# A two-part transformer network on one core: where the modulation rows are summed over the partitions

## What is computed

```python
sc, scc = silu(c), silu(c_ctx)                      # 1024 values each
for l in range(2):
    mod = sc @ w_mod[l] + b_mod[l]                  # 1024 x 6144, a row of 6144 values
    sh1, sc1, g1, sh2, sc2, g2 = split(mod, 6)
    u = rms_norm(h, norm1_g[l]) * (1 + sc1) + sh1
    if l == 0:                                      # the context has its own row
        csh1, csc1, ... = split(scc @ w_mod[l] + b_mod[l], 6)
        uc = rms_norm(ctx, norm1_g[l]) * (1 + csc1) + csh1
    h = h + g1 * mixer(u, uc)
    h = h + g2 * sq_relu_mlp(rms_norm(h, norm2_g[l]) * (1 + sc2) + sh2, w_mlp1[l], w_mlp2[l])
```

## Time and profile before

| | |
|---|---|
| time, median of 3 runs | 1562.83 us (1562.11 to 1563.29) |
| profiled execution, span from first to last instruction | 1560.5 us |
| PE busy | 1523.2 us, 98% |
| DVE busy | 1164.3 us, 75% |
| ACT busy | 785.1 us, 50% |
| POOL busy | 9.6 us, 1% |
| bytes moved by DMA | 311.57 MB, mean 200 GB/s |

### The profile page before, as it was taken

One profiled execution on the slowest core, in us unless ns is written; L12 is line 12 of the kernel. 1 busy time (PEld: TensorE's weight loads), 2 busy tenths in 40 slices (PEclk: granted clock), 3 DMA queues, 4 the chain that ended last, 5 costly groups with the idle time before them and its releaser, 6 DMA issues.

```text
span 1560.5 us, 28953 instructions
## 1 busy us (share of the span) xinstructions
PE 1523.2 (98%) x11842; PEld 1463.9 (94%) x11842; DVE 1164.3 (75%) x1675; ACT 785.1 (50%) x1127; POOL 9.6 (1%) x15
## 2 busy tenths in 40 slices
PE   7999999999999999999989999999999999899998
PEld 7999998999999899999769999987799999899998
DVE  7887788978877858787767877774768887686563
ACT  5444458643435633445765343454654544454542
POOL 0000000000000100000000000000000000000000
PEclk9999999999999999999999999999999999999999
DMA  7656652646664537666233666643345767336540
GB/s 286 230 225 261 228 221 91 243 154 249 226 253 187 226 114 284 250 236 249 81 135 109 263 250 248 247 161 135 102 149 219 268 265 274 136 126 226 189 163 28
DMA packets 43735, 311.57 MB, mean 200 GB/s; under 512 B 4848, under 2 KB 5104, under 8 KB 6512
## 3 DMA queue, kind: packets, MB, share of 16 engines
q1 hardware_dynamic: 42048, 303.33, 51.7%
q0 software_dynamic: 1008, 5.73, 1.0%
q10 hardware_dynamic: 576, 1.05, 0.2%
HBM read 309.05 MB, written 1.05 MB: 199 GB/s over the span
## 4 chain that ended last, share of the span: by engine, by line
PE 67%; DVE 10%; ACT 3%; issue 1%; DVEq 0%; ACTq 0%
PE psum L1822 18%; PE psum L1828 18%; PE psum L1829 18%; DVE w_lo L1025 5%; PE psum L2066 3%; PE psum L2072 3%; PE psum L2071 3%; DVE buf L1034 2%; ACT w_hi L491 2%; PE psum L1899 1%; DVE buf L1195 1%; PE psum L2385 1%; PE psum L2396 0%; PE psum L2315 0%; DVE buf L1198 0%
## 5 line engine op out<-in xcount | busy, mean ns | idle before, releaser
L1822 PE MATMUL psum<-u_hi,w_hi 128*128 128x256 f32 (+1 forms) x2288 | 658.1, 288 | 17.1 <-DVE u_lo L1117 9.6
L1025 DVE TENSOR_TENSOR w_lo<-raw,w_hi 128x1024 fp32r<-128x1024 f32 x480 | 564.5, 1223 | 115.6 <-ACT w_hi L491 115.4
L1828 PE MATMUL psum<-u_lo,w_hi 128*128 128x256 f32 (+1 forms) x2288 | 650.1, 284 | 0.0
L1829 PE MATMUL psum<-u_hi,w_lo 128*128 128x256 f32 (+1 forms) x2288 | 649.9, 284 | 0.0
L491 ACT ACTIVATE w_hi<-raw 128x1024 fp32r<-128x1024 f32 x480 | 477.3, 1046 | 71.0 <-PE psum L1822 59.0
L1822 PEld LDWEIGHTS psum<-u_hi,w_hi 128*128 128x128 f32 x2288 | 440.9, 193 | 21.5 <-DVE w_lo L1025 9.7
L1828 PEld LDWEIGHTS psum<-u_lo,w_hi 128*128 128x128 f32 x2288 | 441.0, 193 | 0.4
L1829 PEld LDWEIGHTS psum<-u_hi,w_lo 128*128 128x128 f32 x2288 | 440.8, 193 | 0.0
L1822 PE MATMUL psum<-hid_hi,w_hi 128*128 128x256 f32 x1220 | 346.2, 284 | 1.8 <-issue 1.2
L1828 PE MATMUL psum<-hid_lo,w_hi 128*128 128x256 f32 x1220 | 345.2, 283 | 0.0
L1829 PE MATMUL psum<-hid_hi,w_lo 128*128 128x256 f32 x1220 | 345.1, 283 | 0.0
(11 more groups left out here) (261 smaller groups left out, 1048.5 us busy)
## 6 DMA issues: line engine op xcount, KB each, us to landing
raw<-stream SPq DMA_DIRECT2D x288, 1024.0 KB, 5.0
buf<-tab POOLq DMA_DIRECT2D x2, 768.0 KB, 5.3
x<-x_in SPq DMA_DIRECT2D x2, 512.0 KB, 6.8
buf<-ctx_in POOLq DMA_DIRECT2D x1, 1024.0 KB, 9.4
buf<-poolmat POOLq DMA_DIRECT2D x1, 1024.0 KB, 5.3
out<-x ACTq DMA_DIRECT2D x4, 256.0 KB, 2.5
cst<-consts POOLq DMA_DIRECT2D x1, 864.0 KB, 9.0
buf<-late POOLq DMA_DIRECT2D x1, 640.0 KB, 4.2
```

The source lines that it names most:

```text
L1025: ve.tensor_tensor(w_lo[:, u], raw[:, u], w_hi[:, u].bitcast(F32), ALU.subtract).then_inc(S.lo_ready, 1)
L1822: ins = te.matmul(dst, w_hi[:, w], hi, start=first, stop=False, skip_group_check=True)
L1828: te.matmul(dst, w_hi[:, w], lo, start=False, stop=False, skip_group_check=True)
L1829: return te.matmul(dst, w_lo[:, w], hi, start=False, stop=last, skip_group_check=True)
```

## The change

The sums over the partitions go from PE to POOL. For each group POOL waits until DVE has accumulated its last unit, makes one `partition_all_reduce` of the accumulator into a new tile `mod_row` (128 x 512, every partition holds the sum), waits for it, and issues a DMA of one row of `mod_row` to 128 partitions, four values each, into `mod`. It waits for the landing before the next sum. Context sums go the same way. So that the four values are neighbours, the columns of the modulation's weight units are stored in another order, and `mod` has another layout. PE's sums and all its waits on the modulation go; DVE's reads of PSUM go, and the bias is added later in seven instructions over many columns (`add_bias`), behind waits for the DMAs. The accumulators alternate from group to group. ACT gets waits before `buf[0]` is overwritten. Constants that nothing uses (`headsum`, `headbc`) go from the program and from the DMA of constants.

```diff
-        MOD_ACC[_g] = _i % 2 if _name == "mlp0" else int(_i >= len(_groups) - 3)
+        MOD_ACC[_g] = _g % 2
...
-CC = {"ident": 0, "ones": 128, "tri": 256, "headsum": 384, "stick": 512, "colmask": 896, "headbc": 960}
-NCONST = CC["headbc"] + NC * P
+CC = {"ident": 0, "ones": 128, "tri": 256, "stick": 384, "colmask": 768}
+NCONST = CC["colmask"] + HD
...
+        mod_row = sb("mod_row", 512)
...
-        mod = mod_t[:, :].rearrange("p (l j c) -> p l j c", l=2, c=2)
+        mod = mod_t[:, :].rearrange("p (l c j) -> p l j c", l=2, c=2)
...
             # POOL
+            def group_sum(acc, done, count, dst, landed, landings):
+                gp.partition_all_reduce(mod_row[:, :], acc, P, bass.bass_isa.ReduceOp.add).then_inc(done, 1)
+                pool.wait_ge(done, count)
+                pool.dma_start(dst, mod_row[0:1, :].rearrange("o (p m) -> o p m", m=4)).then_inc(landed, 16)
+                pool.wait_ge(landed, 16 * landings)
+
+            def sum_groups(name):
+                for g in HOME[name]:
+                    l, at = GROUPS[g][0], 4 * GROUPS[g][1]
+                    pool.wait_ge(S.lo_ready, last_unit(g) + 1)
+                    group_sum(mod_acc[MOD_ACC[g]], S.mod_summed, g + 1, mod[:, l, at:at + 4, 0], S.mod_in, g + 1)
+                    for f in range(2):
+                        if g == CTX_GROUPS[f][-1]:
+                            for n in range(2):
+                                at = 4 * GROUPS[CTX_GROUPS[f][n]][1]
+                                group_sum(ctx_acc[n], S.ctx_summed, 2 * f + n + 1, mod[:, 0, at:at + 4, 1], S.ctx_mod_in, 2 * f + n + 1)
...
+                if name == "ffn0":
+                    sum_groups("ffn0")
                 if name == "ctx":
                     pool.wait_ge(S.acc_ready, 4 * ACC["wout"] + 4)
                     pool.dma_start(buf[3][:, :], ctx_in).then_inc(S.ctx_in, 16)
+                    sum_groups("ffn1")
                 if name == "woe":
+                    sum_groups("ffn2")
+                    sum_groups("ffn3")
                     pool.wait_ge(S.acc_ready, 4 * ACC["ffn3"] + 4)
                     pool.dma_start(buf5[:, 0:NLATE], late).then_inc(S.late_in, 16)
...
+                    sum_groups("mlp0")
...
             # ACT, before the convolution, and before the queries are copied
+            act.wait_ge(S.mod_summed, HOME["ffn0"][-1] + 1)
+            act.wait_ge(S.ctx_summed, 2)
...
+            act.wait_ge(S.mod_summed, HOME["ffn2"][-1] + 1)
...
             # DVE
-                    if j in SUM_AT[name]:
-                        read_modulation(HOME[name][SUM_AT[name].index(j)])
...
-            read_context_modulation(1)
-            modulation_done("ffn1")
-            dve.wait_ge(S.ctx_read, 2)
+            modulation_in(HOME["ffn1"][-1])
+            dve.wait_ge(S.ctx_mod_in, 16 * 4)
+            add_bias(0, 0, 32)
+            add_bias(0, 0, 16, 1)
...
-            modulation_done("ffn3")
+            modulation_in(HOME["ffn3"][-1])
+            add_bias(0, 32, 48)
+            add_bias(1, 0, 24)
...
-            modulation_done("mlp0")
+            modulation_in(HOME["mlp0"][3])
+            add_bias(1, 24, 40)
...
+            modulation_in(HOME["mlp0"][-1])
+            add_bias(1, 40, 48)
             update_x("mlp1", lambda k: part(1, 5, k))
...
             # PE
-                    if j in SUM_AT[name]:
-                        g = groups[SUM_AT[name].index(j)]
-                        sum_modulation(g, 0, last_unit(g))
...
-                if name in ("ffn0", "ffn1"):
-                    sum_context(int(name[3]))
...
-    mods = w["w_mod_2"].reshape(2, 4, 2, P, 12, 512).transpose(0, 4, 1, 3, 2, 5).reshape(-1, P, UNIT)
+    mods = w["w_mod_2"].reshape(2, 4, 2, P, 12, 4, P).transpose(0, 4, 1, 3, 2, 6, 5).reshape(-1, P, UNIT)
```

More of the change, by code:

```diff
@@ L210, in __init__ @@
         self.mod_summed = sem("mod_summed")
-        self.mod_read = sem("mod_read")
+        self.mod_in = sem("mod_in")
+        self.mod_biased = sem("mod_biased")
         self.ctx_summed = sem("ctx_summed")
-        self.ctx_read = sem("ctx_read")
+        self.ctx_mod_in = sem("ctx_mod_in")
         self.dve_chain = sem("dve_chain")
@@ L448, in sum_squares, with last_unit @@
                 gp.tensor_tensor(buf[4][:, 0:T], buf[4][:, 0:T], buf[4][:, T:2 * T], ALU.add).then_inc(S.ctx_ssq, 1)
+            def group_sum(acc, done, count, dst, landed, landings):
[3 more added lines that the diff above has]
+                pool.wait_ge(landed, 16 * landings)
+            def last_unit(g):
+                return max(c for c, (group, _) in MOD_UNIT.items() if group == g)
+            def sum_groups(name):
[8 more added lines that the diff above has]
+                                group_sum(ctx_acc[n], S.ctx_summed, 2 * f + n + 1, mod[:, 0, at:at + 4, 1], S.ctx_mod_in, 2 * f + n + 1)
             pool.wait_ge(S.hi_ready, 4)
@@ L960, in _ @@
             sc.preload_act_table_set("sqrt_and_others")
-            act.wait_ge(S.mod_read, HOME["mlp0"][-1] + 1)
+            act.wait_ge(S.mod_biased, 1)
             shift_operand(1)
@@ L1050, in modulate @@
                 if ctx and q == 0 and f == 1:
-                    dve.wait_ge(S.ctx_summed, 1)
+                    dve.wait_ge(S.ctx_summed, 2)
                 n = CTX_GROUPS[f].index(g) if ctx else None
@@ L1225, in context_operand, with add_bias, modulation_in @@
                                             u_hif[:, k - 1, T:2 * T], ALU.add, ALU.subtract).then_inc(S.ctx_lo, 1)
[L1227 to L1246, removed]
+            def add_bias(l, at, end, c=0):
+                link(ve.tensor_tensor(mod[:, l, at:end, c], mod[:, l, at:end, c],
+                                      prm[:, COL["bmod"] + 48 * l + at:COL["bmod"] + 48 * l + end], ALU.add))
+            def modulation_in(last):
+                dve.wait_ge(S.mod_in, 16 * (last + 1))
             def scale_gain(dst, l, n, gain, c=0):
@@ L1719, in _ @@
             sqrelu("mlp0")
-            modulation_done("mlp0")
+            modulation_in(HOME["mlp0"][3])
+            add_bias(1, 24, 40)
+            dve.sem_inc(S.mod_biased, 1)
             scale_gain("H2", 1, 4, "n2_1")
@@ L1887, in diagonal_block @@
                 ins.then_inc(done, 1)
[L1889 to L1898, removed]
-                    ins = te.matmul(psum[:, bank, at + 2 * m:at + 2 * m + 2], mod_acc[acc][:, m * P:(m + 1) * P],
-                                    ones[:, 0:2], start=m == 0, stop=True, skip_group_check=True)
-                ins.then_inc(S.mod_summed, 1)
-            def sum_context(f):
-                unit_ready(last_unit(CTX_GROUPS[f][1]))
-                pe.wait_ge(S.mod_read, HOME[f"ffn{f}"][-1] + 1)
-                for m in range(8):
-                    ins = te.matmul(psum[:, 6, 8 + 2 * m:10 + 2 * m], ctx_acc[m // 4][:, (m % 4) * P:(m % 4 + 1) * P],
-                                    ones[:, 0:2], start=m == 0, stop=True, skip_group_check=True)
-                ins.then_inc(S.ctx_summed, 1)
             def up(c, i, j, bank, h0):
@@ L1920, in swiglu @@
             def swiglu(name, norm, free=lambda: None):
-                c0, h0, groups = AT[name], STEPS[name], HOME[name]
+                c0, h0 = AT[name], STEPS[name]
                 def down(j, slot, c, i=0, first=False, last=False):
@@ L1952, in swiglu @@
                         down(j - 2, s, c + 3, 2 * i)
-                        if s == 2:
-                            sum_modulation(groups[-3] + i, 1, unit_at(name, "mod", 13), 2 * i)
                 down(FFS - 2, (FFS - 2) % 4, end_of(name) - 2)
-                if name in ("ffn0", "ffn1"):
-                    sum_context(int(name[3]))
                 down(FFS - 1, (FFS - 1) % 4, end_of(name) - 1, last=True)
@@ L1968, in up_pair @@
                         pe.wait_ge(S.up_scaled, h0 + max(j - 1, 3))
-                    if j - 2 in SUM_AT[name]:
-                        pe.wait_ge(S.mod_read, HOME[name][SUM_AT[name].index(j - 2)] + 1)
                     all_k(c, 0, psum[:, bank, 0:TS], w=TS)
@@ L1998, in sqrelu @@
                     down(j - 1)
-                    if j in SUM_AT[name]:
-                        g = HOME[name][SUM_AT[name].index(j)]
-                        pe.wait_ge(S.up_scaled, h0 + j + 1)
-                        sum_modulation(g, MOD_ACC[g], last_unit(g), bank=4 + 2 * (j % 2), at=MOD_COL)
                 down(MLS - 1, last=True)
@@ L2011, in _ @@
             pe.wait_ge(S.ms_ready, NRM["ffn0"] + 1)
-            pe.wait_ge(S.ctx_read, 1)
             def gate_chunk(k, done):
@@ L2107, in _ @@
             pe.wait_ge(S.k_cols_read, 1)
-            pe.wait_ge(S.ctx_read, 2)
             project_tokens("v", 4, lambda b: None, {4: turn_keys})
@@ L2239, in _ @@
                 ins.then_inc(S.acc_ready, 1)
-            pe.wait_ge(S.mod_read, HOME["ffn3"][-1] + 1)
             for k in range(NC):
@@ L2554, in shape_constants @@
     cst[:, CC["tri"]:CC["tri"] + P] = p[:, None] >= p[None, :]
-    for m in range(NC):
```

(4 more changed lines are left out.)

10 lines of the change are left out of this document (removed).

## The result

The changed kernel takes 1565.33 us in the median of 20 runs, the kernel before 1562.89 in 20 runs beside them: ratio 1.0014, 95% interval 1.0008 to 1.0020. That is 2.4 us slower, and lies within the 0.2% that the prediction calls no change; the forecast was 23 us faster. The profiled execution has a span of 1564.0 us, 3.5 more than the earlier trace rows.

A forecast was written before the change was run, and what follows sets the result against it. PE was taken to bound the five stages; its 24.6 us less what DVE takes back gave 23, and 1560.5 - 23 + 2.3 = 1540 us, range 1535 to 1665.

The forecast's parts named there:

- What is removed: PE's 28 sums in the five stages: 0.88 us each, 24.6 us in all.
- What is added on POOL: 28 reductions on POOL at 1.3 to 2 us, each followed by a 2 KB DMA landing after 3 us, hidden.
- the rival of POOL's queue: POOL bounds the kernel from 19 us a sum in the second block; about 2100 us; with longer holds 0.16.
- What the reduction does to DVE: In the five stages, DVE and POOL exclude each other at SBUF; each reduction costs DVE about its hold, 1.3 to 2 us.
- About h us: DVE's loss for each reduction in the five stages, h being how long the reduction holds its input.
- What DVE can spare: Stage length less DVE's busy time and two ACT waits a step: 16.5, 16.5, 19.4, 29.0, 15.3 us in the five stages.
- the prediction's own rule: Each stage's change is the larger of minus PE's share and (sums x h - spare); balance lost at about 3.2 us.
- no gain: Five stages: at holds of 3.0 to 3.3 us PE's 24.6 us return as DVE's waits; 1560 to 1566; chance 0.07.
- DVE becomes the bound: Five stages: holds over 3.2 us make DVE fall behind; 1600 at 4.7, 1662 at 7; chance 0.29 for 3.3 to 7.
- What would show it: Signs in the five stages; right: POOL's sums under 3 us; wrong: subtractions' mean up by tenths, DVE busy over 90%.

## Why the prediction was wrong

*What is removed* was right: every sum shows as -0.88 us, and the run with 16 columns is 25.1 us faster, where 24.6 was worked out. The bias additions are six, not seven, of 0.17 us each.

*What is added on POOL* was too low for the instruction and nearly right for what counts, its hold. The instruction takes 3.22 us, where 1.3 to 2 was taken; it holds DVE for 2.1 of them. The 2 KB row lands 1.9 us after its issue (3 was taken), and no engine waits for POOL anywhere; the rival of POOL's queue fell with that, and with it the estimate of 62 us by the Trainium skill, page "GPSIMD Engine Reference", section "Cross-partition — where GPSIMD wins": this instruction takes a twentieth of it.

*What the reduction does to DVE*: the lock was right, the price too high. "About h us" for each of 28 would be 59; it was 33, because 21 of the sums begin beside a scaling that reads PSUM and a wait for ACT. The prediction had priced no such cover. One unit later, where this cover is gone, the excess was 56 us.

*What DVE can spare* is the step that failed. The prediction took the stage's length less DVE's busy time less "the two waits on ACT that stand in each step"; the earlier trace rows shows the third one, 115.6 us before L1025, and it was left out. In the five stages it is 8.1, 8.6, 11.8, 11.8 and 9.5 us: half of the 97 us counted as spare. What is left besides is partly outside the steps, as the norms at the ends of stages. With the waits for PE alone as spare time, and the excess from the trace (4 x 1.18 + 2 x 2.04 = 8.8 in each of the first two blocks; 3 x 1.18 + 2 x 1.99 = 7.5; 2 x 1.19 + 3 x 0.44 = 3.7; 2.5 + 5 x 0.63 = 5.7), the prediction's own rule gives +0.5, +0.5, +3.0, -4.4 and +2.7, together +2.3 us. The table's first row has -0.5, -0.5, +3.7, -1.2 and +0.8, together +2.3. The sum agrees better than its parts do, and that is in part luck. In the fourth block the rule is 3 us too hopeful, since of its waits for PE all but 4.2 us came behind 930, after the two dearest reductions (882 and 902); that their order is the reason is argued, not tried. In the third block the 8.7 us behind the block's end are left out, and the measured sum contains a slower clock (below) that the rule knows nothing of.

The kernel before with reductions of constants shows that the rule is rough. There the reductions stretch DVE by 7.5, 7.4, 7.5, 3.7 and 5.7 us, of which the rule would make 0, 0, 3.0, 0 and 2.7; the table has +2.4, +2.3, +2.6, +2.7 and +3.8. A part is a wait that the changed kernel doesn't have, of PE's own sums for DVE's accumulation (1.0, 0.9, 1.4 and 1.4 us in the four swiglu blocks), and in the fourth a stretch of the slower clock; but in the first two blocks PE waits 0.9 us each for a subtraction too, where the excess is under the spare time. What is shown, then, is that much less than 97 us was to spare; how much of the waits for PE can be used is open. With 2.1 us for every sum and the right spare time the rule would have given +21, or 1584, the time of the run with later reductions.

A second, smaller part is that a wait of PE can cost more than its length. Behind four gaps in PE's products of 2.1 to 3.4 us (at 733, 905, 1202 and 1342) the granted clock fell to the lower of its two levels, 1.2 GHz; in windows of the changed kernel (us; busy of PE, PEld, DVE, ACT, POOL; clock, where 1.00 is 2.4 GHz):

```profile
738.20:741.50 3.30, 3.30 (x17) 3.30 (x16) 3.02 (x7) 2.86 (x7) 0.00 (x0) 0.50 0.56 238
908.90:912.20 3.30, 3.30 (x17) 3.30 (x17) 2.78 (x5) 0.42 (x1) 0.00 (x0) 0.50 0.93 377
1205.80:1209.10 3.30, 3.30 (x17) 3.30 (x17) 3.30 (x4) 1.25 (x2) 0.00 (x0) 0.50 0.33 89
1345.80:1349.10 3.30, 3.30 (x17) 3.30 (x17) 0.00 (x0) 0.00 (x0) 0.00 (x0) 0.50 0.07 27
```

At 733 two products start 3.38 us apart, 3.26 more than usual, and the step in the pairing is 4.79, so the slow stretch behind it cost about 1.5 us more. The kernel before has one such stretch in these stages, 0.50 from 1198.4 to 1201.7, so three are new: at 1.5 us each an estimate of 4 to 5 us that a sum over DVE's lateness doesn't contain. Behind a gap of 2.14 us at 620 it stayed at 1.00, so the length of the gap alone doesn't say it. This was read from the trace and not tried by itself.

*The rivals.* What came was "no gain", which had 0.07, and not for its reason: its condition was a hold of 3.0 to 3.3 us, the hold was 2.1. "DVE becomes the bound" had the mechanism, but its point of decision, 3.2 us, was worked out from the same wrong spare time: with the waits for PE in its place the rule is in balance at about 1.2 us a sum, and 33.3 / 28 = 1.2 is what a sum cost.

*What would show it*: the subtractions' mean rose by 0.016 us, not by tenths, and DVE was busy 82 to 84% of the first three stages; neither is a sign of "wrong" by the prediction's list. Two of its other marks told: POOL's sums took 3.22 us, where "under 3" was to stand for right, and PE waited 16.9 us for the low halves of weights.

## What to carry to other kernels

Before an engine's idle time is called spare, sort it by what ended it: a wait for a third engine in program order is as spent as work, and at most what it waits for the engine that sets the pace can be given away, and by the runs here not all of that. Work on an idle engine that makes a nearly full one stand is to be placed and cut so that the hold lies under instructions that it doesn't stop: here 256 columns under a read of PSUM and a wait for ACT made the same sums nearly free, 1538.9 in place of 1565.3 us.

## What the runs showed of the hardware

- A reduction over the partitions of 128 x 512 fp32 takes 3.22 us, over 256 columns 1.78, over 16 0.43 in the median, by POOL's records, which are rough. DVE's instructions with two SBUF operands go on 2.1 us after its start, and 0.95 over 256 columns, well before the recorded end. The Trainium skill, page "SBUF — State Buffer", section "Who interferes with whom", says, where it speaks of DVE's two-port modes, that whoever issues first gets the shared pair of ports for the whole instruction, and names DVE's two-input instructions as contending with GpSimd's reads. That the two exclude each other the traces here bear out; that the lock lasts to the end of this instruction they don't.
- Under the hold DVE's scaling out of PSUM kept its 0.68 us, while a tensor_scalar from SBUF to SBUF with one wide operand (L1304) took 2.33 us once, where its median is 0.34.
- Behind four of five gaps of 2.1 to 3.4 us in PE's work in the five stages of the changed kernel the granted clock fell to 0.50, its lower level of 1.2 GHz; behind the fifth, of 2.14 us, it stayed at 1.00.
